# Four slots instead of two for the sample states of a retention layer, two of them in the rows of the next norm's scale and shift

## The reference

```python
RET_HEADS = 4
RET_DK = 256
RET_DV = 512
def retention_scan(q, k, v, s0):          # for a sample S = 1, so one chunk of one row
    ...
    def step(s, qkv):
        qc, kc, vc = qkv
        att = jnp.einsum('bhid,bhjd->bhij', qc, kc) * dmask
        o = jnp.einsum('bhij,bhjv->bhiv', att, vc) + jnp.einsum('bhid,bhdv->bhiv', qc, s) * cross
        s = s * chunk_decay + jnp.einsum('bhjd,bhjv->bhdv', kc * tail, vc)
        return s, o
...
            h = modulate(rmsnorm(x, norm_g[i, 0]), sh1, sc1)
            ...
            x = x + g1[:, None, :] * y
            h = modulate(rmsnorm(x, norm_g[i, 1]), sh2, sc2)
```

## Time and profile before

| What | Value |
|---|---|
| Runs | 4266.0 us median of 3 (4265.8 to 4267.97) |
| Profiled execution | 4266.25 us, its span 4264.7 us |
| PE busy | 3372.4 us (79%) |
| DVE busy | 2486.0 us (58%) |
| POOL busy | 2096.7 us (49%) |
| ACT busy | 690.6 us (16%) |
| Heads | 195 to 895 us of the span |

### The profile page before, as it was taken

One profiled execution on the slowest core, in us unless ns is written; L12 is line 12 of the kernel. 1 busy time (PEld: TensorE's weight loads), 2 busy tenths in 40 slices (PEclk: granted clock), 3 DMA queues, 4 the chain that ended last, 5 costly groups with the idle time before them and its releaser, 6 DMA issues.

```text
span 4264.7 us, 31267 instructions
## 1 busy us (share of the span) xinstructions
PE 3372.4 (79%) x9342; PEld 1367.2 (32%) x9342; DVE 2486.0 (58%) x5918; ACT 690.6 (16%) x1668; POOL 2096.7 (49%) x2213
## 2 busy tenths in 40 slices
PE   6889899889577777777777946996777777777778
PEld 1334333345222222222222334453222222222222
DVE  4324334237866668767843465239666676877643
ACT  2211111111111111111111133111111111111111
POOL 1110100104777767777775300016777767777765
PEclk8799999999899999999999967998999999999999
DMA  9842332417999999999999554139999999999998
GB/s 334 289 138 91 116 126 86 138 50 261 372 409 409 409 393 409 406 398 397 409 407 406 194 73 142 40 116 339 409 409 409 409 392 402 409 403 392 409 409 322
DMA packets 409875, 1293.88 MB, mean 303 GB/s; under 512 B 50094, under 2 KB 73806, under 8 KB 408687
## 3 DMA queue, kind: packets, MB, share of 16 engines
q0 software_dynamic: 309312, 1126.31, 67.4%
q1 hardware_dynamic: 100232, 163.58, 12.1%
q10 hardware_dynamic: 180, 2.18, 0.1%
HBM read 1263.06 MB, written 28.85 MB: 303 GB/s over the span
## 4 chain that ended last, share of the span: by engine, by line
DMA 29%; PE 27%; POOL 19%; DVE 14%; issue 8%; ACT 2%; SPq 1%; POOLq 0%; DVEq 0%; ACTq 0%
DMA arena<-in_peer_v_dram,arena 12%; POOL arena L1356 10%; DMA w<-in_peer_u_dram,arena 10%; POOL w L1356 9%; PE ps L1952 6%; PE ps L1779 4%; PE ps L1871 3%; DVE arena L2316 3%; DMA arena<-in_state_ret_dram 3%; PE ps L1921 3%; PE ps L805 3%; DVE w L2316 3%; DMA w<-in_w_ada_dram 2%; PE ps L697 1%; PE ps L1712 1%
## 5 line engine op out<-in xcount | busy, mean ns | idle before, releaser
L1952 PE MATMUL ps<-arena 128*128 128x512 f32 x3944 | 1943.4, 622 | 644.5 <-DMA arena<-in_peer_v_dram,arena 554.3
L2316 DVE CUSTOM_DVE_ANT_0 w<-w,ps 128x1024 f32<-128x1024 f32 x896 | 1089.8, 1218 | 696.9 <-DMA w<-in_peer_u_dram,arena 695.7
L1952 PEld LDWEIGHTS ps<-arena 128*128 128x128 f32 x3944 | 691.0, 192 | 1872.1 <-DMA arena<-in_peer_v_dram,arena 1221.8
L1356 POOL DMA_INDIRECT arena<-in_peer_v_dram,arena x1040 | 997.2, 959 | 430.4 <-issue 244.9
L1356 POOL DMA_INDIRECT w<-in_peer_u_dram,arena x912 | 862.8, 946 | 280.7 <-issue 246.3
L1609 ACT ACTIVATE arena<-ident,arena 128x128 f32<-128x128 f32 x986 | 377.2, 398 | 1610.0 <-PE ps L1952 1585.3
L1779 PE MATMUL ps<-w,hT 128*128 128x512 f32 x768 | 347.7, 606 | 0.0
L1921 PE MATMUL ps<-hT,w 128*128 128x512 f32 x512 | 275.7, 631 | 1.5 <-ACT hT L1436 1.5
L1317 POOL DMA_DIRECT2D out_dram<-arena x32 | 23.2, 726 | 459.9 <-DVE arena L2088 442.4
L1356 POOL DMA_INDIRECT arena<-in_peer_u_dram,arena x128 | 124.6, 974 | 222.7 <-DVE arena L2248 122.1
L1779 PEld LDWEIGHTS ps<-w,hT 128*128 128x128 f32 x768 | 145.1, 193 | 202.6 <-issue 189.9
(11 more groups left out here) (310 smaller groups left out, 2963.4 us busy)
## 6 DMA issues: line engine op xcount, KB each, us to landing
w<-in_w_ada_dram SPq DMA_DIRECT2D x32, 1024.0 KB, 11.7
w<-in_ret_w_in_dram SPq DMA_DIRECT2D x24, 1024.0 KB, 7.3
out_dram<-arena POOLq DMA_DIRECT2D x36, 512.0 KB, 4.2
arena<-in_peer_v_dram,arena POOLq DMA_INDIRECT x1040, 10.3
x<-in_w_ada_dram SPq DMA_DIRECT2D x16, 1024.0 KB, 11.6
arena<-in_state_ret_dram POOLq DMA_DIRECT2D x32, 512.0 KB, 5.2
w<-in_peer_w_q_dram SPq DMA_DIRECT2D x16, 1024.0 KB, 7.3
w<-in_peer_u_dram,arena POOLq DMA_INDIRECT x912, 10.9
```

Source lines behind the costliest of these rows:

```text
L1356: pool.indirect_dma_start(ring[:, slot, :], None, table, bass.IndirectOffsetOnAxis(ap=index, axis=0)).then_inc(landed_sem[slot], 16)
L1952: mm = pe.matmul(ps[:, bank + half, :], diag[:, n % DIAGS], v_ring[:, n % RING, half * BW:(half + 1) * BW], start=(n % NE == 0), stop=(n % ...
L2316: dve.tensor_tensor_reduce(row, row, h_ps, 1.0, 0.0, ALU.mult, ALU.add, acts[:, j % 2, s:s + 1]).then_inc(u_used, 1)
```

## The change

The states get four slots (`STATES`): the two of `sring`, and the shift row and the scale row of `modp`, 1024 numbers each, cut into 2 x 512. State `b` goes to slot `b % 4`. POOL loads four states ahead; behind the store of state `b` it waits for state `b - 2` to be free and loads state `b + 2` into that slot. The load and store semaphores are the first four of those that the gathers use later, so the gathers' counts start 128 higher in those four. Norm 1's rows can be loaded only after the last head's states have left them, so `modulation(1)` moves from ahead of the last head to behind the key loads of the first mixer, with waits for the stores from slots 2 and 3.

```diff
+STATES = 4
+STATE_TURNS = NS // STATES
...
         sring = cut(2, 2, DV)
+        s_slots = [sring[:, 0], sring[:, 1]] + [modp[:, b, :].rearrange("p (c n) -> p c n", c=2) for b in range(2)]
...
-        s0_ld = [sem("s0_ld0"), sem("s0_ld1")]
-        s1_st = [sem("s1_st0"), sem("s1_st1")]
...
+        s0_ld, s1_st = u_ld[0:STATES], v_ld[0:STATES]
...
-            return 16 * (SLOTS // RING * layer + n // RING + 1)
+            states = HEADS * STATE_TURNS if n % RING < STATES else 0
+            return 16 * (states + SLOTS // RING * layer + n // RING + 1)
...
             sp.wait_ge(mod_st, 16 * LAYERS)
-            sp.wait_ge(h_done, TILES)
-            modulation(1)
             head_blocks(HEADS - 1, True)
...
+                if layer == 0:
+                    for b in (2, 3):
+                        sp.wait_ge(s1_st[b], 16 * HEADS * STATE_TURNS)
+                    modulation(1)
                 query(0)
...
             def head_states(head, last):
+                def follow(b):
+                    if b + STATES < NS or not last:
+                        pool.wait_ge(s1_st[b % STATES], head * STATE_TURNS * 16 + 16 * (b // STATES + 1))
+                        pool.wait_ge(os_ps, head * (NS + 1) + b + 1)
+                        pool.sem_inc(issued, 1)
+                        if b + STATES < NS:
+                            load_state(head, b + STATES)
+                        else:
+                            load_state(head + 1, b + STATES - NS)
+
                 for b in range(NS):
                     pool.wait_ge(s1_done, head * NS + (b + 1))
                     pool.sem_inc(issued, 1)
-                    pool.dma_start(s1(head, b), sring[:, b % 2].unsqueeze(1)).then_inc(s1_st[b % 2], 16)
-                    if b >= 1 and (b < NS - 1 or not last):
-
-                        slot = (b - 1) % 2
-                        pool.wait_ge(s1_st[slot], head * (NS // 2) * 16 + 16 * ((b - 1) // 2 + 1))
-                        pool.wait_ge(os_ps, head * (NS + 1) + b)
-                        pool.sem_inc(issued, 1)
-                        if b + 1 < NS:
-                            load_state(head, b + 1)
-                        else:
-                            load_state(head + 1, 0)
-                if not last:
-                    pool.wait_ge(s1_st[1], head * (NS // 2) * 16 + 16 * (NS // 2))
-                    pool.wait_ge(os_ps, head * (NS + 1) + NS)
-                    pool.sem_inc(issued, 1)
-                    load_state(head + 1, 1)
+                    pool.dma_start(s1(head, b), s_slots[b % STATES].unsqueeze(1)).then_inc(s1_st[b % STATES], 16)
+                    if b >= 2:
+                        follow(b - 2)
+                for b in (NS - 2, NS - 1):
+                    follow(b)
...
-            load_state(0, 0)
-            load_state(0, 1)
+            for b in range(STATES):
+                load_state(0, b)
```

More of the change, by code:

```diff
@@ L1310, in load_state @@
             def load_state(head, b):
-                pool.dma_start(sring[:, b % 2].unsqueeze(1), s0(head, b)).then_inc(s0_ld[b % 2], 16)
+                pool.dma_start(s_slots[b % STATES].unsqueeze(1), s0(head, b)).then_inc(s0_ld[b % STATES], 16)
             def head_states(head, last):
+                def follow(b):
[7 more added lines that the diff above has]
+                            load_state(head + 1, b + STATES - NS)
                 for b in range(NS):
@@ L1351, in _ @@
             head_states(HEADS - 1, True)
-            for s in range(2):
-                pool.wait_ge(s1_st[s], 16 * HEADS * NS // 2)
+            for s in range(STATES):
+                pool.wait_ge(s1_st[s], 16 * HEADS * STATE_TURNS)
             def gather(ring, slot, table, index, landed_sem):
@@ L1796, in state_out @@
                         j = 2 * (b % 2) + c
[L1797 removed]
+                        mm = pe.matmul(ps[32 * j:32 * j + 32, 4, :], qz[:, c, b * NS:b * NS + 32], s_slots[b % STATES][:, c],
                                        start=(b < 2), stop=(b >= NS - 2))
@@ L2080, in head_dve @@
                 for b in range(NS):
-                    dve.wait_ge(s0_ld[b % 2], head * (NS // 2) * 16 + 16 * (b // 2 + 1))
-                    link.link(dve.tensor_scalar(sring[:, b % 2], sring[:, b % 2], cols[:, 3:4], None, ALU.mult))
+                    dve.wait_ge(s0_ld[b % STATES], head * STATE_TURNS * 16 + 16 * (b // STATES + 1))
+                    link.link(dve.tensor_scalar(s_slots[b % STATES], s_slots[b % STATES], cols[:, 3:4], None, ALU.mult))
                     if b == 0:
@@ L2087, in head_dve @@
                     for c in range(2):
-                        ins = dve.scalar_tensor_tensor(sring[:, b % 2, c], vb[:, b % 3], kcol[:, c, b:b + 1],
-                                                       sring[:, b % 2, c], ALU.mult, ALU.add)
+                        ins = dve.scalar_tensor_tensor(s_slots[b % STATES][:, c], vb[:, b % 3], kcol[:, c, b:b + 1],
+                                                       s_slots[b % STATES][:, c], ALU.mult, ALU.add)
                     ins.then_inc(s1_done, 1)
```

## The result

The changed kernel takes 4192.07 us (median of 4 runs, 4191.36 to 4199.97) against 4266.99 for the kernel before (median of 4: the three of the table and one more): a ratio of 0.9827, 95% interval 0.981 to 0.9844. The profiled execution's span is 4190.9 us, 73.8 less.

The account below looks back on a forecast made before the run. PE was taken as the bound at first, a slot's round trip (load, DVE, store, load) at the stretch's end. Plain waits of 57.2 plus slow work of 10.6 make 67.8; 4266.25 - 67.8 = 4198.5 us, range 4190 to 4214.

Parts of the forecast that it names:

- PE's waits for states are the loss, and all of them go: PE's stretch from sixth group to transposes, four heads: 307.80 us become 240.00; 57.2 of the 67.8 are plain waits.
- Length of the stretch with no wait: PE from the sixth group to the transposes, per head: groups, states, parts and sample sum add up to 60.00 us.
- The slow rows go with the idle time: PE's slow work behind the longest wait, state 6 and the next group, returns to full speed: 10.6 us.
- Each state is in time: States in a head: 7 to 21 us early with usual landings, 6 us or more at worst; wait zero.
- The loads of norm 1's rows cost nothing: Norm 1's rows, loaded behind the keys, 58 us ahead of its first instruction: nothing lost.
- Rival A: Reloads slow each other, PE still waits once landings pass 14 us; 4207 to 4257 us, chance 0.13.
- B: Wait was hidden anyway, PE's gap reappears behind the stretch; 4266 us, chance 0.03, shared with Rival A near its upper end.
- C: PE's clock falls to half in a stretch without pauses; 4439 us if in all four stretches, chance 0.02.
- Rival D: PE's shorter idle time helps stages behind, some 8 to 15 us more; 4185 to 4190 us, chance 0.04.

Follow-up runs that it names:

- the longer filler: Kernel before, two slots, with unread PE products added: five full ones ahead of state 5, eight ahead of state 6; 4260.45 against 4266.27 us.
- the filler's first run: Kernel before, two slots, with unread PE products added: four full ones ahead of state 5, six ahead of state 6; 4263.47 against 4263.8 us.

## Why the prediction was right, and where it was off

- *PE's waits for states are the loss, and all of them go.* Right. PE waits for no state, and three slots' timing gives the same stretch, so it is the states' readiness that counts. 4 x 60.00 us were forecast for the stretches; they took 235.54.
- *Length of the stretch with no wait: the step that was mis-sized.* The prediction counted state 5 (0.98), the sample sum (0.95) and state 6 (0.98) one behind the other, 2.91 us. They take 277.59 - 275.76 = 1.83. 1.1 us a head is 4.5 us, the larger part of the 6.4 between 4198.5 and 4192.07; the run with the three apart gives it back. The rest, 1.9 us, is within the drift shown above. (The part behind the heads that the prediction puts at 3200 us is 3370, 4264.7 - 895.)
- *The slow rows go with the idle time.* Right, and shown by the longer filler: clock 1.00, 0.99 and 7.1 us. The prediction priced only two of these rows, 8.6 of its 10.6 us. Behind the wait of 4.75 us state 5 and the sum ran slow too: side by side they took 283.66 + 1.06 - 282.66 = 2.06 us, close to the 1.93 of the prediction, which has them one behind the other at full speed. In the run with late output weights, with no wait, they took 1.04. The kernel before, head 0, granted clock 0.50:

```profile
282.70:284.70 2.00, 2.00 (x6) 0.25 (x6) 0.00 (x0) 0.00 (x0) 1.29 (x2) 0.50 0.07 29
```
- *Each state is in time.* Right, with four times off. Counted from the sixth group, state 3 was done 2.9 us later than forecast, because its row of values came late, which the forecast had not followed. State 4 was 1.8 us later: its reload went out in time and landed after 6.9 us, later than the median. The reloads of states 5 and 6 stand behind the stores of these two, and the states were done 2.0 and 2.3 us later. State 7 was 0.8 us early. The slack of 7 us or more held all of it.
- *The loads of norm 1's rows cost nothing.* Right: 769.20, 57 us ahead of norm 1, and no change when moved alone.
- *Rival A* did not come: reloads land after 5.1 us in the middle and 8.2 at most, against 5.1 and 11.1 before and the 14 at which the chain decides. That transfers can lengthen a reload is shown by the run with reloads one store later, where state 6's reload and the weights meet (8.4 to 10.0 us). Rivals B and C: no gap moved behind the stretch, and the clock is 1.00. Rival D: the stages behind the stretch did not get shorter, beyond drift.
- The prediction took the waits as one cause, the slots. The run with late output weights shows two: 20 us went without a slot. The four slots remove both, since they also move state 5's reload ahead of the weights.

## What to carry to other kernels

Count a ring's slots from the consumer: follow one round trip (issue, landing, update, store) against the time at which the consumer needs the next item, and stop at the number at which nothing is late; here it was three, and the fourth brought nothing. Look also at what else moves when a late item is loaded, since a transfer that can wait is cheaper to move than a slot is to find. And once PE has no gaps, put its narrow products beside each other, those that write to different strips of the output above all.

## What the runs showed of the hardware that was not expected

Narrow products that write to different strips of the output run side by side. A product of 32 columns writes one of four strips of 32 output partitions (`state_out`: `j = 2 * (b % 2) + c`): an even state the first two, two rows in each, an odd state the other two, and the sample sum the first, with two rows. Four rows of one state take 0.98 us, eight rows of two states in all four strips 0.99, and sixteen rows of four states 1.85. State 5, sum and state 6 take 1.83 together against 3.05 apart (3.72 less the waits of 0.67). An estimate from these rows: what counts is the rows in the fullest strip, at 0.44 us each (the sum's two start at 275.77 and 276.21), and some 0.1 once. One state or two make 2 rows there, state 5, sum and state 6 make 4, like four states, and states 4 to 7 with the sum make 6, which took 278.93 - 276.26 = 2.67 us in the run with states four by four. No run changed a state's strip to test it. The Trainium skill (TensorEngine Tiling (Array Packing), Key Properties) says that tiles of the array work independently and that a change of tiling mode drains it. The 0.99 us for two states agree with the first; no run here separates a drain from the rest.

PE's clock fell behind less idle time than the 4.75 and 6.57 us of the earlier trace rows, but not each time. In the filler's first run PE was idle 1.35 and then 2.27 us in head 0, and a state's products behind it took 1.80 us, near twice the 0.98 at 2.4 GHz, as at 1.2 GHz. In head 3 it was idle 1.73 and 2.27 us, and they took 0.98. In the run with reloads one store later it was idle 2.73 us in head 0, and the second row behind it was a group of 8.63 us in place of 7.07; behind 2.40 us in head 3 state 6 took 0.98 and the group 7.1. So the length of the last wait does not tell by itself whether the clock falls. Behind 0.65 and 0.52 us, in the filler's second run, the granted clock was 1.00.
